# Stick-breaking attention of a two-layer trunk: keys moved to the partitions, the sums over later keys moved to matmuls

## The reference, cut to what matters

```
z = einsum('bqhd,bkhd->bhqk', qi, k) * scale
causal = key_pos[None, :] < qpos[:, None]
log_beta = log_sigmoid(z)
log_one_minus = where(causal, log_sigmoid(-z), 0.0)
suffix = cumsum(log_one_minus, axis=3, reverse=True) - log_one_minus
a = where(causal, exp(log_beta + suffix), 0.0)
out = einsum('bhqk,bkhd->bqhd', a, v)
```

## Time and profile before

| | us |
|---|---|
| median of 3 runs | 1921.16 (1919.01 to 1922.81) |
| the profiled execution | 1922.17 |
| its span, first to last instruction | 1920.4 |

### The profile page before, as it was taken

The page is one execution under the profiler, slowest core; times in us unless marked ns, Lnnn a source line. Parts: engine busy times, 40 slices in busy tenths (PEclk is TensorE's granted clock), DMA queues, the critical chain, the costliest instruction groups (busy, mean ns, idle before and its releaser), DMA issues.

```text
span 1920.4 us, 22868 instructions
## 1 busy us (share of the span) xinstructions
PE 1881.3 (98%) x8716; PEld 1539.8 (80%) x8716; DVE 813.3 (42%) x755; ACT 658.8 (34%) x879; POOL 854.3 (44%) x387
## 2 busy tenths in 40 slices
PE   8999999999999999999999999999988999999998
PEld 6888888898888888888888888888754788888887
DVE  7432144524664421445234411445589353412443
ACT  5532222336342312233232312233457342222323
POOL 4443444553444434545434444535344244444442
PEclk9999999999999999999999999999969999999999
DMA  5323322342223233223223233223200222333222
GB/s 179 107 80 95 110 87 77 120 148 66 88 88 107 79 98 110 87 76 120 89 88 103 82 95 113 87 76 117 75 17 1 65 89 90 91 100 111 90 68 85
DMA packets 216924, 175.56 MB, mean 91 GB/s; under 512 B 3166, under 2 KB 215980, under 8 KB 216876
## 3 DMA queue, kind: packets, MB, share of 16 engines
q1 hardware_dynamic: 216876, 174.90, 29.3%
HBM read 172.79 MB, written 2.10 MB: 91 GB/s over the span
## 4 chain that ended last, share of the span: by engine, by line
PE 92%; DVE 4%; issue 2%; ACT 1%; DMA 1%; SPq 0%; POOL 0%; DVEq 0%; ACTq 0%
PE ps L442 29%; PE ps L443 29%; PE ps L444 29%; PE ps L733 1%; PE ps L710 1%; DVE s_sb L1333 1%; DVE z_sb L1319 1%; DMA raw<-in_ffn_w_up_dram 1%; PE ps L592 0%; PE ps L721 0%; DVE ssq L1051 0%; PE ps L603 0%; PE ps L612 0%; ACT w_hi L796 0%; PE ps L652 0%
## 5 line engine op out<-in xcount | busy, mean ns | idle before, releaser
L395 POOL TENSOR_TENSOR w_lo<-raw,w_hi 128x1024 fp32r<-128x1024 f32 (+2 forms) x362 | 811.1, 2261 | 995.7 <-ACT w_hi L796 995.7
L796 ACT ACTIVATE w_hi<-raw 128x1024 fp32r<-128x1024 f32 (+2 forms) x362 | 329.6, 958 | 929.3 <-PE ps L444 923.1
L442 PE MATMUL ps<-u_hi,w_hi 128*128 128x512 f32 x1584 | 620.9, 392 | 4.1 <-DVE u_lo L1298 2.9
L443 PE MATMUL ps<-u_lo,w_hi 128*128 128x512 f32 x1584 | 616.8, 389 | 0.0
L444 PE MATMUL ps<-u_hi,w_lo 128*128 128x512 f32 x1584 | 616.6, 389 | 0.0
L442 PEld LDWEIGHTS ps<-u_hi,w_hi 128*128 128x128 f32 x1584 | 297.6, 188 | 70.2 <-issue 4.9
L444 PEld LDWEIGHTS ps<-u_hi,w_lo 128*128 128x128 f32 x1584 | 297.4, 188 | 62.1
L443 PEld LDWEIGHTS ps<-u_lo,w_hi 128*128 128x128 f32 x1584 | 297.6, 188 | 61.5 <-issue 1.0
L442 PE MATMUL ps<-mid_hi,w_hi 128*128 128x512 f32 x704 | 275.0, 391 | 0.9 <-DVE mid_lo L1051 0.9
L443 PE MATMUL ps<-mid_lo,w_hi 128*128 128x512 f32 x704 | 274.0, 389 | 0.0
L444 PE MATMUL ps<-mid_hi,w_lo 128*128 128x512 f32 x704 | 273.9, 389 | 0.0
(11 more groups left out here) (149 smaller groups left out, 1398.4 us busy)
## 6 DMA issues: line engine op xcount, KB each, us to landing
raw<-in_ffn_w_up_dram SPq DMA_DIRECT2D x44, 1024.0 KB, 5.3
raw<-in_ffn_w_gate_dram SPq DMA_DIRECT2D x43, 1024.0 KB, 5.3
raw<-in_ffn_w_down_dram SPq DMA_DIRECT2D x32, 768.0 KB, 4.8
raw<-in_ffn_w_down_dram SPq DMA_DIRECT2D x32, 640.0 KB, 4.4
raw<-in_a_w_in_dram SPq DMA_DIRECT2D x7, 1024.0 KB, 5.4
raw<-in_w_kv_dram SPq DMA_DIRECT2D x6, 1024.0 KB, 5.0
raw<-in_w_mem_kv_dram SPq DMA_DIRECT2D x4, 1024.0 KB, 5.5
raw<-in_a_w_out_dram SPq DMA_DIRECT2D x4, 1024.0 KB, 5.2
```

The costliest lines, as they stand in the source:

```text
L395: nc.gpsimd.tensor_tensor(w_lo[:, n % 2, part], raw[:, n % 2, part], w_hi[:, n % 2, part].bitcast(F32), ALU.subtract).then_inc(s_wlo, 1)
L442: nc.tensor.matmul(dst, s_hi, m_hi_, start=first, stop=False)
L443: nc.tensor.matmul(dst, s_hi, m_lo_, start=False, stop=False)
L796: nc.scalar.activation(w_hi[:, n % 2, part], raw[:, n % 2, part], ACT.Copy).then_inc(s_whi, 1)
```

## The change

1. **Keys on partitions.** Stationary operand is the keys, moving operand the queries, so the scores come out as [keys, queries]. The transposes, their copy to `aT` and the `z_sb`, `l_sb`, `s_sb` tiles go. The scale moves into the evacuation of the query projection (`queries`).
2. **Pairs of heads, three parts.** A pair is worked on in part A (key blocks 1 and 3: 384 + 128 queries, two heads, 1024 columns), part B (key block 2: 256 queries, two heads, 512 columns, one bank), part C (key block 0: 512 queries, two heads, 1024 columns). A and C take turns in three slots of two banks, B has bank 4, the output bank 5. The two heads' matmuls alternate between rows 0 to 63 and 64 to 127, and the values' between the column halves; in B the two heads are apart.
3. **Mask by matmul.** The diagonal blocks get identity times a mask tile added in PSUM.
4. **Sums over later keys by matmul.** softplus, split into high and low, is multiplied by a triangle of -1 (its own block) and by a full tile of -1 (later blocks), and accumulated onto the scores in PSUM. ACT then takes exp straight from PSUM into `aT`. The scans and POOL's subtraction of 1280 columns go.
5. **Order.** The scores of A and B of the first pair move into the steps of the last input unit, with their first DVE and ACT work. ACT rounds output unit 2 of 4 inside the loop, and POOL's low part of it comes at c == 2. SP no longer waits for the last transpose. The table load for exp and log comes ahead of the memory heads. The first output unit carries only the last pair's C sums and values.

```diff
+            def sb_abs(x, c):                      # DVE
+                dve.wait_ge(s_z[x], c + 1)
+                if c:
+                    dve.wait_ge(s_splo[x], c)
+                nc.vector.tensor_scalar(sp_l[x][:].bitcast(I32), ps_of(x, c).bitcast(I32), 0x7FFFFFFF, None,
+                                        ALU.bitwise_and).then_inc(s_abs[x], 1)
+            def sb_plus(x, c):
+                dve.wait_ge(s_ln[x], c + 1)
+                nc.vector.scalar_tensor_tensor(sp_l[x][:], ps_of(x, c), 0.0, sp_l[x][:], ALU.max,
+                                               ALU.add).then_inc(s_sp[x], 1)
+            def sb_high(x, c):
+                dve.wait_ge(s_sp[x], c + 1)
...
+                nc.vector.tensor_copy(sp_hi[x][c % 2][:], sp_l[x][:]).then_inc(s_sphi[x], 1)
...
+            mem_heads(1, sb_begin)
+            sb_high(A_, 0)
+            sb_high(B_, 0)
+            sb_abs(C_, 0)
+            mem_y(1, MH - 1)
+            for c in range(PAIRS):
+                sb_plus(C_, c)
+                sb_high(C_, c)
+                if c + 1 < PAIRS:
+                    sb_abs(A_, c + 1)
+                    sb_plus(A_, c + 1)
+                    sb_high(A_, c + 1)
+                    sb_abs(B_, c + 1)
+                if c:
+                    sb_y(c - 1)
+                if c + 1 < PAIRS:
+                    sb_abs(C_, c + 1)
+                    sb_plus(B_, c + 1)
+                    sb_high(B_, c + 1)
+            sb_y(PAIRS - 1)
```

```diff
+            def sb_low(x, c):                      # POOL
+                pool.wait_ge(s_sphi[x], c + 1)
+                nc.gpsimd.tensor_tensor(sp_lo[x][c % 2][:], sp_l[x][:], sp_hi[x][c % 2][:].bitcast(F32),
+                                        ALU.subtract).then_inc(s_splo[x], 1)
-            lo_until(0, PLAN.b_out + 2)
...
+            lo_until(0, PLAN.b_out + 1)
+            sb_low(A_, 0)
+            sb_low(B_, 0)
+            for c in range(PAIRS):
+                sb_low(C_, c)
+                if c == 2:
+                    lo_until(PLAN.b_out + 1, PLAN.b_out + 2)
+                if c + 1 < PAIRS:
+                    sb_low(A_, c + 1)
+                    sb_low(B_, c + 1)
```

```diff
+            def sb_dot(dst, c, e, j, first):       # PE
+                rows_ = slice(e * HD, (e + 1) * HD)
+                return nc.tensor.matmul(dst, kT[rows_, c, j * P:(j + 1) * P], q_of(c)[rows_, j * P:],
+                                        start=first, stop=False, skip_group_check=True)
...
+            def both_low(dst, w, x, c, heads, cols):
+                sb_add(dst, w, sp_hi[x][c % 2][:, heads, cols])
+                return sb_add(dst, w, sp_lo[x][c % 2][:, heads, cols])
...
+            def sb_sums_a(c):
+                z = ps_of(A_, c)
+                pe.wait_ge(s_splo[A_], c + 1)
+                for e in range(2):
+                    both_low(z[:, e, :], tri_r[:], A_, c, e, WHOLE)
+                    both_low(z[:, e, 2 * P:3 * P], minus_r[:], A_, c, e, BLOCK3)
+                pe.wait_ge(s_splo[B_], c + 1)
+                for e in range(2):
+                    last = both_low(z[:, e, P:3 * P], minus_r[:], B_, c, e, WHOLE)
+                last.then_inc(s_tri[A_], 1)
+            def sb_sums_b(c):
+                both_low(ps_b, tri_r[:], B_, c, WHOLE, WHOLE)
+                last = both_low(ps_b[:, :, P:], minus_r[:], A_, c, WHOLE, BLOCK3)
+                last.then_inc(s_tri[B_], 1)
+            def sb_sums_c(c):
+                pe.wait_ge(s_sp[C_], c + 1)
+                z = ps_of(C_, c)
+                for e in range(2):
+                    both_low(z[:, e, P:], minus_r[:], A_, c, e, BLOCK1)
+                    both_low(z[:, e, 2 * P:], minus_r[:], B_, c, e, WHOLE)
+                    both_low(z[:, e, 3 * P:], minus_r[:], A_, c, e, BLOCK3)
+                pe.wait_ge(s_splo[C_], c + 1)
+                for e in range(2):
+                    last = both_low(z[:, e, :], tri_r[:], C_, c, e, WHOLE)
+                last.then_inc(s_tri[C_], 1)
...
+            sb_scores_c(0)
+            mem_values(1, MH - 1)
+            pe.wait_ge(s_pylo, 2 * MH)
+            for c in range(PAIRS - 1):
+                sb_sums_a(c)
+                sb_scores_a(c + 1)       # waits exp of C, pair c - 1
+                sb_sums_b(c)
+                if c:
+                    sb_values(c - 1)
+                sb_scores_b(c + 1, 0)    # waits exp of B, pair c
+                sb_scores_c(c + 1)       # waits exp of A, pair c
+                sb_scores_b(c + 1, 1)
+                sb_sums_c(c)
+            sb_sums_a(PAIRS - 1)
+            sb_sums_b(PAIRS - 1)
+            sb_values(PAIRS - 2)
...
+            out_proj(PLAN.b_out, y_ready_b, (lambda: sb_sums_c(PAIRS - 1), lambda: sb_values(PAIRS - 1), nothing, nothing))
```

```diff
+            for c in range(PAIRS):                 # ACT
+                sb_out(A_, c)            # exp from PSUM to aT
+                sb_out(B_, c)
+                if c + 1 < PAIRS:
+                    sb_exp(A_, c + 1)
+                    sb_log(A_, c + 1)
+                if c:
+                    sb_y(c - 1)
+                if c == 1:
+                    hi(PLAN.b_out + 1)
+                if c + 1 < PAIRS:
+                    sb_exp(B_, c + 1)
+                    sb_log(B_, c + 1)
+                    sb_exp(C_, c + 1)
+                sb_out(C_, c)
+                if c + 1 < PAIRS:
+                    sb_log(C_, c + 1)
+            sb_y(PAIRS - 1)
```

More of the change, by code:

```diff
@@ L197, in trunk_program, with two @@
         mem_junk = place("mem_junk", [P, D], r_rms + 2048)
-        s_sb = [place("s_sb0", [P, ZW], r_u + 25600), place("s_sb1", [P, ZW], r_rms)]
+        sp_l = [place("sp_l_a", [P, 2, T], r_tmp), place("sp_l_b", [P, 2, UC], r_rms),
+                place("sp_l_c", [P, 2, T], r_rms + 2048)]
+        def two(name, shape, offsets, dt=F32):
+            return [place(f"{name}{q}", shape, at_, dt) for q, at_ in enumerate(offsets)]
+        sp_hi = [two("sp_hi_a", [P, 2, T], (r_u, r_u + 4096), F32R),
+                 two("sp_hi_b", [P, 2, UC], (r_u + 16384, r_u + 18432), F32R),
+                 two("sp_hi_c", [P, 2, T], (r_u + 24576,), F32R) * 2]
+        sp_lo = [two("sp_lo_a", [P, 2, T], (r_u + 8192, r_u + 12288), F32R),
+                 two("sp_lo_b", [P, 2, UC], (r_u + 20480, r_u + 22528), F32R),
+                 two("sp_lo_c", [P, 2, T], (r_u + 28672,), F32R) * 2]
+        aT = [two("aT_a", [P, 2, T], (r_tmp + 4096, r_tmp + 8192)),
+              two("aT_b", [P, 2, UC], (r_mem + 4096, r_mem + 6144)),
+              two("aT_c", [P, 2, T], (r_mem,)) * 2]
         small = region(0.5)
@@ new lines, in sb_scores_b, with sb_scores_c @@
+            def sb_scores_b(c, e):
+                if e:
+                    pe.wait_ge(s_zb0, c + 1)
+                elif c:
+                    pe.wait_ge(s_a[B_], c)
+                last = sb_dot(ps_b[:, e, :], c, e, 2, not e)
+                if e:
+                    last = sb_add(ps_b[:, :, 0:P], ident_r[:], mask_r[:].unsqueeze(1).to_broadcast([P, 2, P]))
+                last.then_inc(s_z[B_] if e else s_zb0, 1)
+            def sb_scores_c(c):
+                if c:
+                    pe.wait_ge(s_a[A_], c)
+                else:
+                    pe.wait_ge(s_evac, PLAN.b_in + 4)
+                z = ps_of(C_, c)
+                for e in (1, 0):
+                    sb_dot(z[:, e, :], c, e, 0, True)
+                for e in (1, 0):
+                    last = sb_add(z[:, e, 0:P], ident_r[:], mask_r[:])
+                last.then_inc(s_z[C_], 1)
@@ new lines, in _ @@
+            BLOCK1, BLOCK3, WHOLE = slice(0, 3 * P), slice(3 * P, T), slice(None)
+            def sb_sums_a(c):
+                z = ps_of(A_, c)
+                pe.wait_ge(s_splo[A_], c + 1)
[3 more added lines that the diff above has]
+                pe.wait_ge(s_splo[B_], c + 1)
+                for e in range(2):
+                    last = both_low(z[:, e, P:3 * P], minus_r[:], B_, c, e, WHOLE)
+                last.then_inc(s_tri[A_], 1)
@@ new lines, in sb_values @@
+            def sb_values(c):
+                for x in (A_, B_, C_):
+                    pe.wait_ge(s_a[x], c + 1)
+                if c:
+                    pe.wait_ge(s_bylo, c)
+                for j, (x, cols) in enumerate(((C_, WHOLE), (A_, BLOCK1), (B_, WHOLE), (A_, BLOCK3))):
+                    for e in range(2):
+                        h = 2 * c + e
+                        last = nc.tensor.matmul(ps_y[e * HD:(e + 1) * HD, j * P:], vB[:, j, h * HD:(h + 1) * HD],
+                                                aT[x][c % 2][:, e, cols], start=j == 0, stop=j == TT - 1)
+                last.then_inc(s_bv, 1)
@@ new lines, in sb_y, with sb_begin @@
+            def sb_y(c):
+                act.wait_ge(s_bv, c + 1)
+                nc.scalar.activation(y_hi[:, c, :], ps_y, ACT.Copy).then_inc(s_byhi, 1)
+            def sb_begin(part):
+                if part == 3:
+                    sb_exp(A_, 0)
+                    sb_log(A_, 0)
```

(19 more changed lines are left out.)

239 lines of the change are left out of this document (98 added, 141 removed).

## The result

| | us |
|---|---|
| median after, 4 runs | 1900.2 (1899.37 to 1900.52) |
| median before, the runs beside it | 1921.56 |
| ratio after to before | 0.9891, 95% interval 0.9876 to 0.9905 |
| profiled execution after, and its span | 1899.37, 1897.6 |

A repeat later gave 1899.29, ratio 0.9881 [0.9866, 0.9896]; one run of the kernel before beside it took 3823 us and is left out. The kernel is 1.1% faster, and the stage is cut as forecast; what the forecast had too much of is above all the term for the clock.

A forecast was written before the change was run, and what follows sets the result against it. DVE was taken to bound the stick-breaking stage, 7.04 us a head against PE's 5.9. Profiled 1922.2 - 22.6 (shorter stage) + 6 (half clock) = 1905.6; with the median 1.0 below, 1905, range 1894 to 1920.

The forecast's parts named there:

- end: From the last pair's start to the first output unit's end: remaining sums, values and output unit matmuls, 20.7 us.
- clock: In the changed stage, 10 to 20 us at half clock, about 0.4 of it lost: 6 us added.
- What bounded before: Stick-breaking stage before: DVE bounds at 7.04 us a head against PE's 5.9; low clock made first heads dearer.
- The ring: Loop's chain of waits through part B: 7.8 us on PE, 5.2 through DVE and POOL, period 13.0.
- The factor of 0.62 for alternated halves: f32 matmuls alternating between array halves take 0.62 of their time in sequence.
- PE's work: PE's matmuls for a pair of heads after the change: 11.2 us, against 11.8 before.
- DVE and ACT: Work for a pair of heads after the change: DVE 8.6 us, ACT 8.8 us.
- Round three: Loop round with POOL's weights, 4.7 us, between C(2) and A(3); 2.2 of it left over, round 15.2 us.
- rival 4: Clock holds, so no 6 us lost; and 128-column matmuls cost 0.05 less each: time 1896, chance 0.15.
- rival 1: Alternated matmul halves don't overlap: 3.3 us more a pair, some 19 us, time 1924, chance 0.06.
- rival 2: PE stays at half clock in the loop, period 22.4 instead of 13.0 us: time 1932, chance 0.09.
- rival 3: Loop period 15.3 instead of 13.0 us, with copies meeting POOL's subtractions each round: time 1916, chance 0.17.

The follow-up runs named there:

- e7: Kernel before without abs(z) on DVE, ACT taking the exp of 0 times z instead: 1913.49 us, ratio 0.9957.
- e5: Kernel before with useless 512-column matmuls added in heads 0 to 4 to keep PE from idling: 1922.95 us, ratio 0.9999.
- e2: Changed kernel with a pair's values done one head after the other instead of alternating: 1906.54 us, ratio 0.9919.
- e12: e1 with part B's low half taken by DVE instead of POOL from the second pair on: 1895.72 us, ratio 0.9864.
- e6: e1 with values moved behind the scores of B and C, DVE's and ACT's steps reordered to match: 1912.02 us, ratio 0.9948.
- e1: Changed kernel with POOL's low part of output unit 2 moved from round three to behind the loop: 1897.21 us, ratio 0.9868.
- e3: Changed kernel without part C's sums over later key blocks (12 matmuls a pair): 1905.0 us, ratio 0.9901.

## Why the prediction was right, point by point

Rounds are counted here on PE, from one B part of sums A to the next.

| step | predicted | measured |
|---|---|---|
| end of the last input unit | 1398.7 | 1399.1 |
| from there to the first B part of sums A | 6.4 | 6.36 |
| rounds one to five | 11.9, 13.0, 15.2, 13.0, 13.0 | 12.15, 12.96, 14.06, 14.36, 12.96 |
| sum of the rounds | 66.1 | 66.5 |
| end | 20.7 | 20.0 |
| output unit at DVE, without the clock | 1491.9 | 1491.92, with the clock |
| clock | +6 | +1.4 |

- *What bounded before.* DVE, as said, and `e7` and `e5` show it for the heads. That the low clock made the first heads dearer fell: about 1 us. What I missed is the clock behind the heads, where PE is last: some 2.7 us at 1484.38, which the change took away without my counting it. It is no error in the sum, which starts from the time measured before.
- *The ring.* Predicted 7.8 on PE and 5.2 from B's scores to PE; measured 1466.86 - 1458.98 = 7.9 and 1471.94 - 1466.86 = 5.1. What ends PE's wait is POOL's low half of B, as named. `e2` and `e12` lengthen and shorten it and the rounds follow, one for one upward, downward until A's low half is next.
- *Sizes inside the 7.8.* Two errors cancel. Values were 2.75, measured 2.31; the scores of B, C, B with masks were 2.1, measured 2.70, which includes shape changes of which I had put 0.5 on the ring as a whole. Scores A 1.3 and 1.4; sums B 0.7 and 0.8; the B part of sums A 0.5 and 0.67. That the ring came out within 0.1 is luck in part. The factor of 0.62 for alternated halves was not held to either: A was summed with about 0.56 and the values with 0.60.
- *PE's work.* 11.2 predicted, 11.93 measured, mostly the same shape changes. What of this lies on the ring is in the 7.9 above; the rest lies in the wait and cost nothing.
- *DVE and ACT.* 8.6 and 8.8 predicted, 8.42 and 8.45 measured.
- *Narrow matmuls.* 128 columns of fp32r take 0.06 and 0.11 in turn (1467.45, 1467.51, 1467.62); I had 0.11 for each.
- *Round three.* 15.2 predicted, 14.06 measured. POOL's weights took 5.16 in place of 4.7 and PE's wait was 1.8. I had left 2.2 over; 1.1 was. The 5.16 are 2.36 and 2.84: DVE's copy `sp_hi_a` (1437.64, 0.71) lay across the start of the second instruction. Round four is 1.4 longer, by the clock.
- *The copy beside POOL.* 1.52 against 0.43 in round three, where it was expected, and not in the others. The Trainium skill, SBUF — State Buffer, section "Who interferes with whom", has POOL and DVE's two-port copies exclude each other; this trace agrees (1.52, and 2.10 in `e6`).
- *The clock, the term that was off.* I took 10 to 20 us at half clock, each costing 0.4. There were 3.4, costing 1.4, in the round behind PE's longest wait. The term should have been 1.4; with it the forecast is 1900.4 instead of 1905. I read its size off the kernel before, where PE had no work to fill DVE's time. After, each wait is 1 us between 12 us of work. That is rival 4's first half. Rivals 1, 2 and 3 did not come; but `e6`, with rounds of 15.18, shows that rival 3's 15.3 was one change of DVE's order away.
- *The rest, where luck helped.* That 1900.4 is so close is luck. Without the clock the sum was 1.4 too long (round three and the end 1.8, the start and round one 0.6 the other way). Against it stands the step from the profiled execution to the median: I took 1.0 off, and the median lies 0.8 above.

Open: why round two of `e1` has the low clock that the changed kernel has in round four, how `e3`'s later rounds would stand at full clock, and what a kernel before the change would gain with full clock at its last values alone.

## What to carry to other kernels

When no engine is full in a steady round, find the wait that recurs once a round and walk back from it; what lies on that ring counts one for one, and what lies in the wait may be free or, where it keeps TensorE busy, better than free. Before moving work off the ring, find the next bound: the queue order of every other engine makes a ring, and the busiest engine's own work is one; here they stood 0.3 to 0.4 us behind the first. Where another engine is full with a margin (7.04 against 5.9 us here), a low clock on TensorE costs next to nothing, and mending it gains as little; where TensorE is the last on the path, as at the end of the stage before, it costs in full (4.50 us for values that take 2.34).
